# A hybrid decoder layer in float32: order and size of the first loads, two gains folded into the output weights, maxima ahead of query splits, four early weight splits, and 60 unused transposes on TensorE

## The reference

```
z, xbc, dt, q, k, v = split(rms(x) @ w_in)
xbc   = silu(causal_conv4(xbc) + conv_b)
y_ssd = rms(ssd_scan(xbc, dt) * silu(z)) * ssd_norm_w      # 512 columns
y_dif = rms(sum over keys of (softmax1 - lam*softmax2) v) * subln_w * 0.2   # 4 heads of 128
x1 = x  + rms(concat(y_ssd, y_dif) @ w_out) * norm_mix_post
x2 = x1 + rms(cross_attention(rms(x1), rms(mem))) * norm_mem_post    # 4 heads, 256 memory tokens
x3 = x2 + rms(square(relu(rms(x2) @ w_up)) @ w_down) * norm_mlp_post
```

## Time and profile before

| | before |
|---|---|
| three runs, us | 1492.48, 1492.92, 1497.02 (median 1492.92) |
| profiled execution, us | 1498.33, of which the span 1496.6 |
| TensorE (PE) busy | 1448.0 us, 97% of the span |
| VectorE (DVE) busy | 938.3 us, 63% |
| ScalarE (ACT) busy | 681.2 us, 46% |
| mean granted TensorE clock | 0.991 |

### The profile page before, as it was taken

One profiled execution on the slowest core, in us unless ns is written; L12 is line 12 of the kernel. 1 busy time (PEld: TensorE's weight loads), 2 busy tenths in 40 slices (PEclk: granted clock), 3 DMA queues, 4 the chain that ended last, 5 costly groups with the idle time before them and its releaser, 6 DMA issues. The chain is left out here.

```text
span 1496.6 us, 21242 instructions
## 1 busy us (share of the span) xinstructions
PE 1448.0 (97%) x7956; PEld 1229.4 (82%) x7956; DVE 938.3 (63%) x1600; ACT 681.2 (46%) x1391; POOL 87.0 (6%) x132
## 2 busy tenths in 40 slices
PE   7999999998998999999999999999999999999998
PEld 5889999995668988888888777888888788888886
DVE  5783566637885524522632688887777585557798
ACT  6324222336885523523532565445444364454443
POOL 1000000000010001100000352000000000000012
PEclk9999999998999999999999999999999999999999
DMA  8111111111002631110011242564443598776463
GB/s 321 50 38 57 29 30 29 35 43 66 1 1 85 200 110 29 57 57 29 2 57 57 99 150 83 198 228 161 153 155 127 203 340 285 237 240 191 156 232 127
DMA packets 95333, 177.56 MB, mean 119 GB/s; under 512 B 9600, under 2 KB 34304, under 8 KB 93184
## 3 DMA queue, kind: packets, MB, share of 16 engines
q1 hardware_dynamic: 89536, 152.05, 29.9%
q10 hardware_dynamic: 5696, 24.15, 5.0%
HBM read 138.42 MB, written 37.75 MB: 118 GB/s over the span
## 5 line engine op out<-in xcount | busy, mean ns | idle before, releaser
L2064 PE MATMUL ps<-wh,oph 128*128 128x256 f32 (+2 forms) x768 | 249.0, 324 | 0.3 <-ACT mprobs L1072 0.3
L2065 PE MATMUL ps<-wl,oph 128*128 128x256 f32 (+2 forms) x768 | 244.9, 319 | 0.0
L2066 PE MATMUL ps<-wh,opl 128*128 128x256 f32 (+2 forms) x768 | 244.9, 319 | 0.0
L2064 PE MATMUL ps<-d_ring 128*128 128x512 f32 x448 | 175.4, 391 | 2.4 <-DVE d_ring L1938 2.4
L2066 PE MATMUL ps<-d_ring 128*128 128x512 f32 x448 | 175.2, 391 | 0.0
L2065 PE MATMUL ps<-d_ring 128*128 128x512 f32 x448 | 174.8, 390 | 0.0
L2064 PEld LDWEIGHTS ps<-wh,oph 128*128 128x128 f32 x768 | 145.0, 189 | 11.1 <-ACT mprobs L1072 0.5
L2066 PEld LDWEIGHTS ps<-wh,opl 128*128 128x128 f32 x768 | 145.1, 189 | 10.9
L2065 PEld LDWEIGHTS ps<-wl,oph 128*128 128x128 f32 x768 | 145.2, 189 | 10.4
L731 POOL TENSOR_TENSOR rms<-stat,mhalf 128x1 f32<-128x1 f32 (+2 forms) x59 | 50.7, 864 | 1358.5 <-DVE stat L1317 1337.2
L1234 ACT ACTIVATE d_ring<-left_raw 128x512 fp32r<-128x512 f32 x112 | 70.3, 628 | 100.9 <-PE ps L2066 78.0
(11 more groups left out here) (348 smaller groups left out, 2936.8 us busy)
## 6 DMA issues: line engine op xcount, KB each, us to landing
right_raw<-in_w_down_dram SPq DMA_DIRECT2D x128, 256.0 KB, 3.8
u_kept_s<-us SPq DMA_DIRECT2D x64, 256.0 KB, 2.5
left_raw<-u_kept_s SPq DMA_DIRECT2D x64, 256.0 KB, 2.8
w_blk<-in_w_up_blocks_dram ACTq DMA_DIRECT2D x14, 1024.0 KB, 5.7
left_raw<-u_kept_a SPq DMA_DIRECT2D x48, 256.0 KB, 3.3
raw<-in_w_in_dram SPq DMA_DIRECT2D x18, 512.0 KB, 3.7
u_kept_a<-u SPq DMA_DIRECT2D x24, 256.0 KB, 2.3
x_in<-in_x_dram SPq DMA_DIRECT2D x8, 512.0 KB, 8.6
```

The costliest lines, as they stand in the source:

```text
L2064: te.matmul(o, lh, rh, start=first, stop=False)
L2065: te.matmul(o, lh, rl, start=False, stop=False)
L2066: return te.matmul(o, ll, rh, start=False, stop=last)
```

## The change

Parts, in the order of the program:

- The first loads are cut and reordered. ScalarE's queue issues only gain_t and two single slices of x transposed ahead of its first instruction; the two small loads come later. The first half of each weight unit is loaded, split and waited for in two quarters (256 KB, two slices k). The other slices of x transposed go to SyncE's queue, between the weights.
- TensorE makes 40 transposes of `ident` into an unused bank after its wait for `ident`, and ahead of its wait for the first data (`WARM`). It makes 20 more in attention between the scores of step 1 and those of step 2 (`KEEP`).
- The gains ssd_norm_w and subln_w leave `y_norm` and `o_norm` and are multiplied into the rows of w_out where its halves are split: two instructions of 512 columns instead of one of 1024, on ScalarE and on VectorE. `o_norm` becomes one instruction instead of four.
- In cross-attention, from step 2 on (and in step 0 as before), VectorE makes the maxima of n ahead of the low part of the queries of n+1. The banks of the scores change places, so that the scores of step 1 don't wait for the last copy of the query projection (15 of 16 instead of 16).
- At the start of the MLP, the four weight splits stand at step 28 on both engines (before: ScalarE at 28 and 30, VectorE at 30 and 31), and `mlp_norm(4)` moves from step 30 to 31, behind `mo_resid(6)`.

```diff
+FIRST_PART = (slice(0, 512), slice(512, 1024), slice(1024, 2048))
+WARM = 40
+KEEP = 20
...
-    return 2 * (n % 2) if n else 6
+    return 2 * ((n + 1) % 2) if n else 6
...
+        def row_gains(q):
+
+            if q // 2 < UNIT0["mq"]:
+                first = 4 * (q // 2 % 2) + 2 * (q % 2)
+                return [(slice(k * 512, (k + 1) * 512), gain_o[:, first + k:first + k + 1]) for k in range(2)]
+            return [(slice(k * UC, (k + 1) * UC), gain_q[:, 4 * (q % 2) + k:4 * (q % 2) + k + 1]) for k in range(4)]
...
             load_first(0, 0)
             load_first(1, 0)
             load_first(0, 1)
             load_first(1, 1)
+            load_xt(1, 0)
+            load_first(0, 2)
+            load_first(1, 2)
+            load_xt(2, 0)
+            load_xt(3, 0)
             x_tile(0)
             x_tile(1)
...
-                if UNIT0["mq"] <= q // 2 < UNIT0["mo"]:
-                    for k in range(4):
-                        c = slice(k * UC, (k + 1) * UC)
-                        ins = s.activation(wh[:, slot, part][:, c], raw[:, q % 2, c], ACT.Copy, scale=gain_q[:, 4 * (q % 2) + k:4 * (q % 2) + k + 1])
+                if UNIT0["wo"] <= q // 2 < UNIT0["mo"]:
+                    if q == 2 * UNIT0["wo"]:
+                        act.wait_ge(lam_s, 2)
+                    for c, gain in row_gains(q):
+                        ins = s.activation(wh[:, slot, part][:, c], raw[:, q % 2, c], ACT.Copy, scale=gain)
...
-                if st in (28, 30):
-                    quad_hi(st - 28)
-                    quad_hi(st - 27)
+                if st == 28:
+                    for n in range(4):
+                        quad_hi(n)
...
-                v.scalar_tensor_tensor(y, y, rms[:, COL[("y", i)]:COL[("y", i)] + 1], ssd_w[:].rearrange("p (k c) -> p k c", k=4),
-                                       ALU.mult, ALU.mult)
+                v.tensor_scalar(y, y, rms[:, COL[("y", i)]:COL[("y", i)] + 1], None, ALU.mult)
...
-                for h in range(DH):
-                    o = mix[:, 4 + h, i * P:(i + 1) * P]
-                    ins = v.scalar_tensor_tensor(o, o, rms[:, COL[("o", i)] + h:COL[("o", i)] + h + 1], sub_w[:], ALU.mult, ALU.mult)
-                ins.then_inc(h_ready, 1)
+                o = mix[:, 4:8, i * P:(i + 1) * P]
+                v.tensor_tensor(o, o, rms[:, COL[("o", i)]:COL[("o", i)] + DH].unsqueeze(2).to_broadcast([P, DH, P]), ALU.mult).then_inc(h_ready, 1)
...
-                if 1 <= n < NT - 1:
-                    query_lo(n + 1)
+                if n == 1:
+                    query_lo(2)
...
-                if n == 0:
-                    query_lo(1)
+                if n != 1 and n + 1 < NT:
+                    query_lo(n + 1)
...
-                if st in (22, 24, 25, 26, 30):
-                    mlp_norm((22, 24, 25, 26, 30).index(st))
+                if st in (22, 24, 25, 26, 31):
+                    mlp_norm((22, 24, 25, 26, 31).index(st))
...
-                if st in (30, 31):
-                    quad_lo(2 * (st - 30))
-                    quad_lo(2 * (st - 30) + 1)
+                if st == 28:
+                    for n in range(4):
+                        quad_lo(n)
...
+                for n in range(WARM):
+                    te.transpose(ps[:, 7, 0:P], ident[:], ident[:])
...
+                if n == 2:
+                    for _ in range(KEEP):
+                        te.transpose(ps[:, 6, 0:P], ident[:], ident[:])
                 if n < NS:
                     scores(n)
...
+                if n == 2:
+                    pe.wait_ge(ev["mq"], 16)
...
-            pe.wait_ge(ev["mq"], 16)
+            pe.wait_ge(ev["mq"], 15)
```

More of the change, by code:

```diff
@@ L364, in build @@
         lam = small("lam", [P, 8])
-        sub_w = small("sub_w", [P, P])
+        gain_o = small("gain_o", [P, KD])
         stat = small("stat", [P, N_COLS])
@@ L547, in load_half, with load_first, load_xt @@
                 sp.dma_start(raw[:, q % 2, half_slot(q)[2]], src).then_inc(raw_loaded[q % 2], 16)
-            def load_first(u, half):
-                src = unit_source("xbc", u, half)
-                if half:
+            def load_first(u, part):
+                src = unit_source("xbc", u, part // 2)
+                if part == 2:
                     sp.dma_start(raw_b[u][:], src).then_inc(rawb_loaded[u], 16)
                 else:
-                    sp.dma_start(raw[:, u, 0:UE // 2], src).then_inc(raw_loaded[u], 16)
+                    sp.dma_start(raw[:, u, part * 512:(part + 1) * 512],
+                                 src[:, 2 * part:2 * part + 2, :]).then_inc(raw_loaded[u] if part else first_loaded[u], 16)
+            def load_xt(n, half):
+                cut = slice(512 * half, 512 * half + 512)
+                sp.dma_start(xt_raw[:, 2 * n:2 * n + 2, cut],
+                             t["xT"][n * 256:(n + 1) * 256, cut].rearrange("(k p) c -> p k c", p=P)).then_inc(xt_loaded[4 * half + n], 16)
             def x_tile(i):
@@ L837, in _ @@
             act.wait_ge(gain_t_loaded, 16)
-            in_hi(0, 0)
-            first_hi(1, 0)
-            for k in range(1, 4):
+            for k in range(4):
                 in_hi(k, 0)
-            first_hi(0, 1)
-            first_hi(1, 1)
-            for k in range(4, KD):
+                if k < 3:
+                    first_hi((k + 1) % 2, (k + 1) // 2)
+            act.dma_start(pos_i[:], t["positions_t"]).then_inc(rows_loaded, 16)
+            act.dma_start(conv_wb[:], t["conv_t"]).then_inc(rows_loaded, 16)
+            first_hi(0, 2)
+            in_hi(4, 0)
+            first_hi(1, 2)
+            for k in range(5, KD):
                 in_hi(k, 0)
@@ L1305, in split_lo @@
                 slot, part, n = half_slot(q)
-                if UNIT0["mq"] <= q // 2 < UNIT0["mo"]:
-                    for k in range(4):
-                        c = slice(k * UC, (k + 1) * UC)
-                        ins = v.scalar_tensor_tensor(wl[:, slot, part][:, c], raw[:, q % 2, c], gain_q[:, 4 * (q % 2) + k:4 * (q % 2) + k + 1],
-                                                     wh[:, slot, part][:, c].bitcast(F32), ALU.mult, ALU.subtract)
+                if UNIT0["wo"] <= q // 2 < UNIT0["mo"]:
+                    for c, gain in row_gains(q):
+                        ins = v.scalar_tensor_tensor(wl[:, slot, part][:, c], raw[:, q % 2, c], gain, wh[:, slot, part][:, c].bitcast(F32),
+                                                     ALU.mult, ALU.subtract)
                     ins.then_inc(w_lo, 1)
@@ L1333, in normalise, with first_lo @@
                 v.scalar_tensor_tensor(dst, src, rms[:, COL[what]:COL[what] + 1], gain, ALU.mult, ALU.mult).then_inc(h_ready, 1)
-            def first_lo(u, half, n):
-                dve.wait_ge(w_hi, n)
-                part = (slice(None), u, slice(half * 1024, (half + 1) * 1024))
-                v.tensor_tensor(wl[part], raw_b[u][:] if half else raw[:, u, 0:UE // 2], wh[part].bitcast(F32),
-                                ALU.subtract).then_inc(w_lo, 1)
+            def first_lo(u, part):
+                dve.wait_ge(w_hi if part else first_hi_done, 2 * max(part - 1, 0) + u + 1)
+                cut = FIRST_PART[part]
+                v.tensor_tensor(wl[:, u, cut], raw_b[u][:] if part == 2 else raw[:, u, cut], wh[:, u, cut].bitcast(F32),
+                                ALU.subtract).then_inc(w_lo if part else first_lo_done, 1)
             def in_lo(k, half):
```

56 lines of the change are left out of this document (28 added, 28 removed).

## The result

The changed kernel takes 1476.62 us (median of 4 runs, 1476.01 to 1477.39) against 1494.46 for the kernel before in the same comparison: a ratio of 0.9884, 95% interval 0.9864 to 0.9904, 17.3 us with 14.3 to 20.3. The forecast was 1480.5, in 1474 to 1488: faster, as forecast, and 3.9 us faster than the number. The gain itself, 17.8 us between these two medians, was forecast as 12.4, from a median of 1492.9. The profiled execution took 1477.13 us (span 1475.4), the one before 1498.33 (span 1496.6), so 21.2 us lie between the two traces.

What follows compares the result with a forecast made beforehand. TensorE, 97% busy, bounds the kernel by its waits, work and clock. Gains 3.8 + 3.0 + 0.5 + 5.0 + 2.8 = 15.1 us, less 2.7, make 12.4 off the 1492.9 median: 1480.5 us, range 1474 to 1488.

Steps and rivals of the forecast that it cites:

- the terms of the norms: `o_norm` and `y_norm` on VectorE: shorter norms save at least 3.6 us there, mostly beside other work, so 0.5 us (0 to 2).
- a step of cross-attention: Cross-attention: a step of 8.38 us falls to 7.4 to 7.6, TensorE becoming the bound, gaining 0.83 to 0.95 us.
- the cap at the start: Step 4's last slice of x, ready at 34.6 and set by loads, allows at most 0.9 us beyond the 3.8.
- The first rival: Start and attention: transposes don't wake the clock, all 40 run slow, 8.0 us gained in all, 1484.9 us; chance 0.20.
- The start: Beginning: earlier data and 40 transposes raising the clock put the first matmul at 8.6, at full clock; gain 3.8 us.
- Attention: Scores of steps 2 and 3: 20 transposes keep the clock up through the 2.94 us wait; gain 3.0 us (0 to 4.0).
- The 2.7 us: Whole kernel: about half the 5.4 us between profiled execution and median, laid to low clock, can't be won again; taken off 15.1.
- Cross-attention: Cross-attention: low part of the queries leaves the ring, five waits give 3.9 to 4.8, banks 0.7; 5.0 us (3.5 to 5.5).
- The banks: Start of cross-attention: the bank exchange removes the 0.7 us wait on the last copy of the query projection.
- The MLP: Start of the MLP: the 3.36 us wait for weights goes, a 2.2 us wait on `h_tok` comes; gain 2.8 us.
- the 1.1: Start of the MLP: gain remaining if the new 2.2 us wait makes the clock fall as before, instead of 2.8 us.

## Why the prediction was right, and where it was off

*The sum.* The forecast's stages add up to 15.1 us, the two traces differ by 21.2. Of the 6.1 us between them, 1.6 lie in cross-attention, 1.4 in attention, 3.1 in three stages that were put at nothing, and 0.1 less at the start and more at the MLP cancel. Each part gained by the mechanism forecast. Mis-sized were the terms of the norms (0.5 for 2.1) and of a step of cross-attention (0.83 to 0.95 for 1.06), and what was wrong is the cap at the start.

*The first rival: do transposes wake the clock?* They do, in ten traces out of ten that have them at the beginning: the clock rose each time before the first other matmul, and in the four without them it rose only 3.4 to 5.6 us behind it. The forecast gave this rival 0.20; before the result, only mixed work was to be seen in the trace.

*The start, 3.8 forecast, 3.7 measured: the size right by luck.* The forecast had data at 7.9, and the rise of the clock at 6.9 from one example. In ten traces the rise came between 4.36 and 7.67, and the 40 transposes ended accordingly, so that the first matmul of the seven with 40 and the smaller load came at 7.30 to 8.90, median 8.39 (forecast 8.6). What failed is the cap: I took the loads for what sets step 4's last slice, and a ready time that does not change. It is ScalarE's squares, one ahead of each copy, and in the changed kernel one of them waited for x until 24.79 (before: until 23.78), so the last slice moved from 33.85 to 34.88. That is why the transposes, 2.8 us alone in the kernel before, bring little in the changed one: the first stage ended at 41.73 to 42.28 in five traces with the 40, and at 42.09 and 42.53 in the two without.

*Attention, 3.0 for the clock and 0.5 for the norms; measured 3.4 and 1.5.* With the transposes and the old norms the stage takes 104.34 and 104.36, in two kernels that are otherwise different, and 104.97 in a third, where the wait for the exponentials left behind the 20 transposes was 1.42 us instead of 0.75; with the new norms 102.80. The clock's 3.4 is within the bounds given (0 to 4.0). In all ten traces with these transposes there is no low stretch behind the wait, in all four without there is one, of 3.4 to 10.2 us. So the forecast's 3.0 was the price of a long one; a stretch of 3.4 us cost the stage 1.1. The norms' term was mis-sized. I took their saving on VectorE, which is 0.45 us for a norm and not the 0.6 of the forecast, for covered. Set beside the run with the old norms, TensorE's transposes of `probs` come sooner at four places, each behind one of the first four norms, by 0.31, 0.19, 0.45 and 0.18 us, and by 0.27 at 355 us, behind the last `y_norm`. There VectorE was the late one, and what it saved reached TensorE.

*Behind attention, 0 forecast, 1.7 and 0.6 measured.* The kernel before had a low stretch of 6.8 us at 452.5, the changed one 3.4 us at 444.7; without one the stage takes 10.74 in the kernel before with the 40 transposes and in the changed kernel with the old norms, and 10.15 with the new ones. So 0.6 of the 1.7 is the norms': two more such places, of 0.45 and 0.15 us, lie behind the last scores. With the 1.5 ahead they are worth 2.1 us, not 0.5. The other 1.1 is the clock. Of the 0.6 in the keys and values 0.5 are back in the run with the old norms and splits (114.09); the rest is not traced. The stretches differ between executions of like kernels, and those 1.1 us are luck of the two traces: it went into the difference of the traces, 21.2, and not into that of the medians, 1494.46 - 1476.62 = 17.8. The 2.7 us that the forecast took off for this were 3.4.

*Cross-attention, 5.0 forecast, 6.6 measured.* The mechanism is the one forecast, and waits on `opl` are gone. The size was off because I counted the five waits of the list at 0.83 to 0.95 each. The seven intervals between the products with `vm` were 8.20, four of 8.38, 7.83 and 7.20 before, and 7.42, four of 7.32, 7.21 and 7.20 after. So the full step became 7.32, not 7.4 to 7.6, and gave 1.06 where the list shows 0.83. From the start of the last matmul ahead of the wait to the start of the product it was 1.11 us before and is 0.12 after: 0.99, of which the list leaves out what the modelled end of that matmul covers. The other 0.07 lie in the product itself. And the sixth interval gave 0.6, for a small wait on `mprobs` that I had not counted. The banks gave 1.0 where their wait was 0.7, likely for the same reason.

*The MLP, 2.8 forecast, 2.9 measured,* by the steps given: wait of 2.11 on `h_tok` (forecast 2.2) and no fall of the clock. That the clock did not fall was in part luck: it fell at this wait in two of eight traces, and there 1.3 us were gained, near the 1.1 that the forecast named for that case.

*w_down, 0 forecast, 0.8 measured.* Both traces have a low stretch of 3.4 us there, over different work. Executions without one took 305.2 to 305.7, so it cost the changed kernel's 0.7 to 1.2. These 0.8 us are luck of the two traces, as the 1.1 behind attention.

What stays open: how much the 60 transposes are worth in the changed kernel. By the stages of single executions up to 3, by the medians 0.35, and the intervals hold both. And why the longest load of w_mk takes 6.2 to 6.5 us in two traces, 5.2 and 5.6 in two (with waits of 0.4 and 0.7 us), and at most 4.9 in the other ten, with no wait above 0.2: what makes them long is not shown.

## What to carry to other kernels

A gain at a stage's beginning is worth only what the stage's last input allows: before counting it, look up which engine, not only which load, delivers that input, and what it does first. A list of waits gives less than a wait is worth, since the last matmul's modelled end covers part of it; take the interval between like instructions in a loop and compare it with TensorE's own work. And unused transposes can pay only where the clock falls behind a long wait, and only if no later wait takes the gain: the 20 alone shortened attention by 2.75 us in their trace and the kernel before by nothing in its median. How many are right is set by the time at which the real data comes, for 40 of them ended up to 1.7 us after it.

## What was not expected of the hardware

Unused float32 transposes alone raise TensorE's clock, and when it rises varies: from a start at 1.63 us each time, at 4.36, 5.55, 5.91, 5.92, 6.29, 6.42, 6.64, 6.84, 7.26 and 7.67 us in ten kernels, whose beginnings differ in little. Without them, matmuls alone from 7.32, 7.38, 9.71 and 9.95 raised it at 11.9, 10.79, 13.85 and 15.57. The same 2.9 us wait in attention was followed by a low stretch of 10.2, 10.2, 6.8 and 3.4 us, and a wait of 2.1 us at the MLP by one in two traces of eight. Apart from such stretches the stages with like code agree from trace to trace (the 85.91 us of w_mo in all, the 265.1 of w_up, from the first product with `t2h` to the last with `t4h`, within 0.06), so that a difference of stages can be read from single traces, and a difference in the clock can't.
